# Strassen's seven block products for the feed-forward's gate and value, in a two-layer encoder kernel

## The reference

```python
h = layer_norm(DEEPNORM_ALPHA * h + m, ln_mix_g[layer], ln_mix_b[layer])   # m ends with "... @ w_out"
gate, up = jnp.split(h @ ffn_w_in[layer], 2, axis=-1)                      # w_in: 1024 x 5632
f = (jax.nn.silu(gate) * up) @ ffn_w_out[layer]                            # w_out: 2816 x 1024
h = layer_norm(DEEPNORM_ALPHA * h + f, ln_ffn_g[layer], ln_ffn_b[layer])
```

## Time and profile before

| | us |
|---|---|
| median of 3 runs | 2858.58 (2857.2 to 2860.23) |
| the profiled execution: its own time | 2860.23 |
| its span, first to last instruction | 2858.4 |
| PE busy (modelled) | 2659.3, 93% of the span |
| mean granted clock of PE | 0.963 of full speed |

### The profile page before, as it was taken

How to read it: one execution, slowest core, us unless ns; L and a number is a source line. 1 busy time by engine, 2 the same in 40 slices (tenths; PEclk the granted TensorE clock), 3 DMA queues, 4 the chain that set the end, 5 groups by cost and what they waited for, 6 DMA issues and landing times. The chain is left out here.

```text
span 2858.4 us, 34971 instructions
## 1 busy us (share of the span) xinstructions
PE 2659.3 (93%) x13476; PEld 2226.2 (78%) x13476; DVE 1420.3 (50%) x2523; ACT 556.6 (19%) x825; POOL 617.5 (22%) x448
## 2 busy tenths in 40 slices
PE   6787789999999999978999999995999999999996
PEld 5676678788888888767888888885878888888875
DVE  8699526532333322382667766666552333333227
ACT  3223232111111111112222222321211111111110
POOL 2968311111111121111111111110111111112210
PEclk9898899999999999989999999997999999999998
DMA  4333324112111111012010111101411121111101
GB/s 135 86 102 100 83 74 133 59 45 59 44 44 44 44 44 59 15 59 58 23 38 28 31 37 31 35 7 52 140 59 45 45 58 44 44 44 44 46 14 59
DMA packets 207701, 157.96 MB, mean 55 GB/s; under 512 B 15616, under 2 KB 189824, under 8 KB 206720
## 3 DMA queue, kind: packets, MB, share of 16 engines
q1 hardware_dynamic: 207616, 156.81, 18.0%
HBM read 139.02 MB, written 17.76 MB: 55 GB/s over the span
## 5 line engine op out<-in xcount | busy, mean ns | idle before, releaser
L588 DVE TENSOR_TENSOR h<-h,ps 128x512 f32<-128x512 f32 x320 | 219.5, 686 | 200.0 <-PE ps L365 199.6
L347 PE MATMUL ps<-aT_hi,w_hi 128*128 128x512 f32 x704 | 279.6, 397 | 3.0 <-DVE aT_lo L561 3.0
L347 PE MATMUL ps<-aT_hi,w_lo 128*128 128x512 f32 x704 | 277.5, 394 | 0.0
L347 PE MATMUL ps<-aT_lo,w_hi 128*128 128x512 f32 x704 | 275.1, 391 | 0.0
L1738 PE MATMUL ps<-aT_hi,w_hi 128*128 128x512 f32 x640 | 256.9, 401 | 1.7 <-PEq L241 1.7
L1738 PE MATMUL ps<-aT_hi,w_lo 128*128 128x512 f32 x640 | 251.5, 393 | 0.0
L1738 PE MATMUL ps<-aT_lo,w_hi 128*128 128x512 f32 x640 | 250.0, 391 | 0.0
L1710 POOL TENSOR_TENSOR w_lo<-w_raw,w_hi 128x1024 fp32r<-128x1024 f32 x38 | 91.7, 2419 | 555.7 <-ACT w_hi L62 555.7
L571 DVE TENSOR_TENSOR hgo_act_out<-hgo_act_out,ps 128x512 f32<-128x512 f32 x44 | 30.2, 687 | 352.5 <-ACT hgo_act_out L460 352.5
L571 DVE TENSOR_TENSOR s5o_act_out<-s5o_act_out,ps 128x512 f32<-128x512 f32 x44 | 30.2, 687 | 350.7 <-ACT s5o_act_out L460 350.7
L347 PEld LDWEIGHTS ps<-aT_hi,w_lo 128*128 128x128 f32 x704 | 133.2, 189 | 31.3
(11 more groups left out here) (324 smaller groups left out, 5919.4 us busy)
## 6 DMA issues: line engine op xcount, KB each, us to landing
w_raw<-in_ffn_w_in_dram SPq DMA_DIRECT2D x44, 512.0 KB, 5.0
w_raw<-in_hg_w_in_dram SPq DMA_DIRECT2D x40, 512.0 KB, 4.0
s5o_raw<-in_ffn_w_in_dram SPq DMA_DIRECT2D x22, 512.0 KB, 5.0
s5o_raw<-in_ffn_w_out_dram SPq DMA_DIRECT2D x11, 1024.0 KB, 5.2
hgo_raw<-in_ffn_w_in_dram SPq DMA_DIRECT2D x22, 512.0 KB, 5.0
hgo_raw<-in_ffn_w_out_dram SPq DMA_DIRECT2D x11, 1024.0 KB, 5.1
h<-in_x_dram SPq DMA_DIRECT2D x4, 1024.0 KB, 9.0
s_w_raw<-in_s_w_in_dram SPq DMA_DIRECT2D x8, 512.0 KB, 4.8
```

The lines of the kernel that those rows point to most:

```text
L347: ins = t.matmul(ps[:, 2 * b + a, :], w[q][:, a, kk, :], x[:, kk, rows], start=(kk == 0 and m == 0), stop=(kk == KT - 1 and m == 2))
L588: v.tensor_tensor(part, part, ps[:, 4 + m % 4, :], ALU.add).then_inc(S["out_acc"], 1)
```

## The change

Each hidden tile's gate and value is written as a 2x2 by 2x2 block product: weights by (gate or value, upper or lower four channel blocks), tokens by (channel half, token half). Seven block products of 12 matmuls replace the eight. `PRODUCTS` lists for each: first and second weight block with their operation, the token set, the PSUM bank (0 to 3).

- **Weights.** Each product has a set of its own: for the five sums, SP loads both blocks (256 KB each) into one of five slots (`SLOT_AT`), POOL adds or subtracts them, ACT makes the hi part, POOL the lo part; for the two plain ones ACT and DVE do it. Every load of a slot waits for the product that read it last. `w_out` comes as 512 KB for each tile, and DVE makes its lo part.
- **Tokens.** Five sums or differences of token blocks are made when a pair is turned (`keep_pair`): DVE forms them, ACT their hi parts, POOL their lo parts. Pairs are now token tiles (p, p + 4). The first product waits for all 20 lo parts.
- **Merging.** Ten DVE operations (`merge`) and three ACT copies (`keep`) a tile put the seven products together as banks come free; silu runs in place in SBUF. The hidden hi part moves from POOL to ACT.
- **Order.** A body of the loop is the products of tiles 2i+1 and 2i+2, then the outputs of group i. The last tile (21) stays at 96 matmuls, from six sets loaded during the last full outputs.
- **S5 stage.** On SP, `ungroup_y(n - 1)` comes behind `regroup_u(n + 1)`.

The core of the diff (of the three `body` functions the first is ACT's, the second DVE's, the third POOL's):

```diff
+    PRODUCTS = [((0, 0), (1, 1), ALU.add, "11+22", 0), ((1, 0), (1, 1), ALU.add, "11", 1),
+                ((0, 0), (0, 1), ALU.add, "22", 2), ((1, 1), None, None, "21-11", 3),
+                ((0, 0), None, None, "12-22", 0), ((0, 1), (1, 1), ALU.subtract, "21+22", 1),
+                ((1, 0), (0, 0), ALU.subtract, "11+12", 2)]
...
+    SLOT_AT = [0, 1, 2, 3, 4, 0, 1, 2, 3, 4, 0, 1, 2, 3]
...
+            def load_set(i, pos):
+                f, r = tile_at(i, pos)
+                if used_last(i, pos) is not None:
+                    s.wait_ge(S["product"], used_last(i, pos) + 1)
+                    carry(s, i)
+                fetch(plain_rows(pos), PRODUCTS[r][0], PRODUCTS[r][1], f, S[f"set_in{SLOT_AT[pos]}"])
...
+            turn_pair(PAIRS - 1)
+            t.wait_ge(S["x_set_lo"], 5 * PAIRS)
+            t.wait_ge(S["lo"], 2 * PAIRS)
+            unit(-1, 1)
...
+            def keep(f, n):
+                a.wait_ge(S["product"], f * NP + n + 1)
+                carry(a, f)
+                if n == 2:
+                    a.wait_ge(S["merged"], f * NMERGE + 4)
+                    carry(a, f)
+                elif not (isinstance(f, int) and f == 0):
+                    a.wait_ge(S["hid"], 2 * f)
+                    carry(a, f)
+                a.activation(act_out[0 if n == 0 else 1][:, :], ps[:, n, :], ACT.Copy).then_inc(S["kept"], 1)
...
+            def body(i):
+                hidden_hi(2 * i, 0, i)
+                w2_split(i, 0)
+                keep(2 * i + 1, 0)
+                keep(2 * i + 1, 1)
+                set_hi(i, 5)
+                keep(2 * i + 1, 2)
+                set_hi(i, 6)
+                w2_split(i, 1)
+                silu_late(2 * i + 1)
+                set_hi(i, 7)
+                silu_early(2 * i + 1)
+                set_hi(i, 8)
+                set_hi(i, 9)
+                hidden_hi(2 * i + 1, 1, i)
+                keep(2 * i + 2, 0)
+                keep(2 * i + 2, 1)
+                for pos in range(10, 13):
+                    set_hi(i, pos)
...
+            def body(i):
+                split_w2(i, 0)
+                merge_steps(2 * i + 1, range(1, 5))
+                split_w2(i, 1)
+                merge_steps(2 * i + 1, range(5, 11))
+                set_lo(i, 10)
+                merge(2 * i + 2, 1)
+                set_lo(i, 11)
+                merge_steps(2 * i + 2, range(2, 11))
+                accumulate(i, slice(0, 4))
...
+            def make_set(i, pos):
+                f, r = tile_at(i, pos)
+                g.wait_ge(S[f"set_in{SLOT_AT[pos]}"], 32 * uses(i, pos))
+                carry(g, i)
+                (hi, lo), (one, other) = set_rows(pos), plain_rows(pos)
+                g.tensor_tensor(other, one, other, PRODUCTS[r][2]).then_inc(S["set_sum"], 1)
+                g.wait_ge(S["set_hi"], index(i, pos) + 1)
+                carry(g, i)
+                g.tensor_tensor(lo, other, hi.bitcast(F32), ALU.subtract).then_inc(S["set_lo"], 1)
...
+            def body(i):
+                hidden_lo(2 * i, 0)
+                for pos in (5, 6, 7, 8, 9):
+                    make_set(i, pos)
+                hidden_lo(2 * i + 1, 1)
+                make_set(i, 12)
+                make_set(i, 13)
+                if not (isinstance(i, int) and i == LAST - 1):
+                    for pos in range(3):
+                        make_set(i + 1, pos)
...
                 if n == 0:
                     put_u(2)
-                else:
-                    ungroup_y(n - 1)
                 if 1 <= n < KT - 1:
                     regroup_u(n + 1)
+                if n >= 1:
+                    ungroup_y(n - 1)
```

More of the change, by code:

```diff
@@ L204, in project_and_feed @@
[L204 to L208, removed]
+    block_of = [k.first[:, :], k.hi0[:, :], k.lo0[:, :]] + [sb(f"x{n}", [P, PIECE], F32R)[:, :] for n in (3, 4, 5)]
+    plain_block = {n: k.plain[f"{tag}_x{n}"][:, :] for n in (3, 4, 5)}
@@ L498, in _ @@
-            if turns:
-                for tt in range(2, NT):
-                    keep_turned(NT + tt, tt)
+            for pos in range(NP, NP + 3):
+                set_hi(-1, pos)
+            for pair in range(PAIRS):
+                keep_pair(pair)
+            set_hi(-1, 10)
+            set_hi(-1, 11)
+            keep(0, 0)
+            keep(0, 1)
+            set_hi(-1, 12)
+            keep(0, 2)
+            set_hi(-1, 13)
+            silu_late(0)
+            set_hi(0, 0)
+            silu_early(0)
@@ new lines, in _ @@
+            body(0)
+            with a.Fori(1, LAST - 1) as i:
+                body(i)
+            body(LAST - 1)
+            for n, (_, second) in enumerate(LAST_SETS):
+                if second is not None:
+                    a.wait_ge(S["last_sum"], LAST_SUMS[n])
+                else:
+                    a.wait_ge(S[f"last_in{n}"], 32)
+                rows, raw_rows = last_set(n)
+                split_hi(a, rows[:, 0, :], raw_rows[:, 1, :]).then_inc(S["last_hi"], 1)
+            hidden_hi(2 * LAST, 0, LAST)
@@ L502, in _ @@
+            if turns:
+                for n in range(NT):
+                    keep_turned(n)
         @block.vector
@@ L620, in _, with body @@
-            group(0)
-            with v.Fori(1, NG - 2) as i:
-                group(i)
-            group(NG - 2)
-            product(LAST, 1)
+                    keep_pair(pair - 1)
+            keep_pair(PAIRS - 1)
+            set_lo(-1, 10)
+            set_lo(-1, 11)
+            merge_steps(0, range(1, 11))
+            set_lo(0, 3)
+            set_lo(0, 4)
+            def body(i):
+                split_w2(i, 0)
[7 more added lines that the diff above has]
+                accumulate(i, slice(0, 4))
+                if not (isinstance(i, int) and i == LAST - 1):
+                    set_lo(i + 1, 3)
+                    set_lo(i + 1, 4)
+                accumulate(i, slice(4, NT))
@@ L639, in _ @@
             if turns:
[L640 to L641 removed]
+                for n in range(4, NT):
+                    keep_turned(n)
         @block.gpsimd
@@ new lines, in _ @@
+            body(0)
+            with g.Fori(1, LAST - 1) as i:
+                body(i)
+            body(LAST - 1)
+            for n, (_, second) in enumerate(LAST_SETS):
+                (hi, lo), (one, other) = ([a[:, m, :] for m in range(2)] for a in last_set(n))
+                if second is not None:
+                    g.wait_ge(S[f"last_in{n}"], 32)
+                    g.tensor_tensor(other, one, other, ALU.add).then_inc(S["last_sum"], 1)
+                g.wait_ge(S["last_hi"], n + 1)
+                g.tensor_tensor(lo, other, hi.bitcast(F32), ALU.subtract).then_inc(S["last_lo"], 1)
```

628 lines of the change are left out of this document (371 added, 257 removed).

## The result

The changed kernel took 2912.01 us (median of 4 runs, 2908.02 to 2914.64) against 2857.89 for the kernel before (4 runs, 2854.99 to 2860.23): ratio 1.0189, 95% interval 1.0171 to 1.0206. It is 54 us slower; forecast were 2888 and "slower", with a range up to 2925. The profiled execution took 2908.02 us (span 2906.2), 47.8 more than the profiled one of before; all that follows accounts for these 47.8.

The account below looks back on a forecast made before the run. PE was taken to bound feed-forward groups, VectorE and PE both the middle norm. Layer 1 +14.5, layer 0 +17.0 and S5 -2.2 made +29.3 on the profiled 2860.2, giving a median of 2888 us; range 2843 to 2925.

Parts of the forecast that it names:

- turn of pair 0 to first product: Norm in the middle: first product waits for all token work and starts at 56.7 us, plus 1.4 for a slow turn.
- nine bodies: Feed-forward loop of each layer: nine periods of 64.3 us, against 65.8 before.
- last tile: End of outputs 9 to second outputs: shorter by 4.5 us in layer 0 and 7.0 in layer 1.
- The clock: Norm in the middle: longer PE idling slows a turn by 1.4 us and later products by about 2, +3.5 a layer.
- the walk: One loop body step by step: sets 7, 8, 9 each 0.6 us late, set 10 2.2 late; 60.3 becomes 64.3.
- The hand-overs: Between POOL and ACT in a summed set's round: about 0.08 us each, round 3.34; bounds 0.04 or 0.15.
- S5: S5 stage: regroup_u issued earlier shortens one PE wait, gaining 2.2 us once, bounds 0 and 3.
- The 9.4 us a layer for the exclusion: DVE operations with two SBUF inputs and POOL's sums block each other; without that each layer would be 9.4 us shorter.
- the short operations: Rival, faster: POOL's operations take 1.06 us, a body 62.6, total 2844; chance 0.13 together with all sets in time.
- the DMA rival: Rival, slower: loads of 512 KB a product set the pace, a body takes 68.6 us, total 2980; chance 0.06.
- the even case: Rival, about even: hand-overs and port waits at their low end, 14 us less a layer, total 2859; chance 0.12.
- All sets in time: Rival, faster: no product waits, 4.0 us more gained a body, some 2805; chance 0.13 together with the short operations.

Follow-up runs that it names:

- e3: Changed kernel with only POOL's order altered: in the body it sums the next set before making the rest of the current one; 2862.37 us.
- e4: Changed kernel with only ACT's order altered: roundings of plain sets 10 and 11 put ahead of the two keep copies; 2883.43 us.
- e8: Changed kernel without the five token sums, plain token blocks in their place (other values result); 2881.33 us.
- e6: As e5, with DVE's rest of w2 for the second tile moved behind merge 10; 2826.92 us, ratio to the kernel before 0.9886.
- e2: Changed kernel without POOL's weight sums in the loop's sets, all loads kept (other values result); 2832.24 us.
- e5: Changed kernel with the POOL order of e3, the ACT order of e4, and set 7's rounding ahead of a silu; 2823.31 us, ratio to before 0.988.
- e1: Changed kernel with the S5 stage's DMA order put back, ungroup_y ahead of regroup_u; 2916.08 us.
- e10: As e5, with the S5 stage's old DMA order put back; 2827.12 us, ratio to the kernel before 0.9888.
- e7: As e6, with DVE instead of POOL making two of the last pair's five token rests; 2818.58 us, ratio to the kernel before 0.9858.
- e9: As e5, with DVE instead of POOL making two of the last pair's five token rests; 2820.52 us, ratio to the kernel before 0.9866.

## Why the prediction was right, and by how much it was short

The direction was right, slower, and the time lies in the range; the size was short, +29.3 us against +47.8. By its steps, in the profiled execution:

| step | forecast | layer 0 | layer 1 |
|---|---|---|---|
| turn of pair 0 to first product, clock included | 58.1 | 57.3 | 57.4 |
| first product to first outputs, clock included | 69.0 | 70.5 | 67.6 |
| nine bodies | 578.7 | 586.5 | 586.5 |
| end of outputs 9 against before | +21.5 | +31.4 | +27.3 |
| last tile | -4.5 / -7.0 | -1.4 | -6.4 |

(The clock's 3.5 a layer is put in as 1.4 and 2.1.) 31.4 - 1.4 + 27.3 - 6.4 = 50.9, less 2.4 for an earlier begin of layer 0's feed-forward, leaves 48.5; measured were 47.8, so all else is 0.7 shorter. Forecast was 29.3. The prediction also took layer 1's 706.0 for both layers, where layer 0 had 704.6 before; that is 1.4 of the 18.5 missing.

**The step that was short is the body: 64.3 said, 65.1 measured.** Nine bodies in each layer make 15.6 us of the missing 18.5. The mechanism of the walk held, its sizes were short. A stall costs its shown idle time and 0.27, so in the body shown above set 7 cost 1.18, sets 8 and 9 0.73 and 0.70, and set 10 2.30, where the walk had 0.6, 0.6, 0.6 and 2.2.

*Set 7, the largest part.* The walk let DVE's rest of w2 end 16.4 us into the body and the set be ready at 19.8. The rest ended at 16.80 (2519.03) and the set was ready at 20.15 (2522.38), 3.35 later, as walked. PE began 0.13 behind that, a hand-over that the walk put at nothing. So the product started 1.06 late. The 0.4 lie in the steps in front of w2's rest: set 6 was ready at 15.7, not 15.2. The slower restart of PE, 0.11, is the rest of the 1.18, and of what set 10 cost over 2.2.

*The hand-overs.* 0.08 was estimated, 0.12 to ACT and 0.17 back were measured, so the round is 3.44 to 3.50, not 3.34; the upper bound of 0.15 was nearly it. Sets 8 and 9 cost the round less PE's 2.75, 0.7 each. Their restarts come not on top of that, since a later start of PE also makes it want the next set later.

*The clock.* The prediction charged it to the middle alone (turn 1.9 and first 48 matmuls 2.05 measured, 1.4 and 2 said). It also fell in one body a layer, 1.6 each, and within the first three tiles, for 10.2 us in layer 0 and 3.4 in layer 1; no step had either. That goes with the 2.9 us by which layer 0's first tiles took longer, of which 0.45 are longer waits; no run separates the two. Against that stands the ninth body, 63.95, in which the six last sets take the place of the next body's.

**Held by the traces:** POOL's operations at 1.27 to 1.32 for a set in the body, but for the sum that DVE held; the mechanism of both late places (e3 for the round, e4 for ACT's order, in part); the first product at 57.4, where 56.7 and 1.4 for the clock were said, of which e8 gives 14.8 to the token sums; outputs covered; the last tile in layer 1.

**The last tile in layer 0** gained 1.4 instead of 4.5. The second outputs were said to begin at 50.1 and began at 52.03 behind the end of outputs 9, and the kernel before began them at 53.4, not at the 54.6 that was worked back from an add. Most of the 1.9 is a slow turn again, in PE's timeline of the changed kernel:

```profile
1263.72 1.91 PE L416 MATMUL ps<-ident,h 128*128 128x128 f32 x16
...
1272.61 3.65 PE L416 MATMUL ps<-ident,h 128*128 128x128 f32 x16 [6.99 <-DVE aT_lo L772]
```

A turn behind 6.99 us of idle PE takes 3.65, where the one in front of it took 1.91. The prediction gave the slow turn to the middle alone. The clock was also at 0.50 for 3.4 us at the tile's begin, around a wait of 3.42 us. In e6 it wasn't, and with the same slow turn e6's second outputs began at 50.70, 1.3 sooner. So by estimate the clock took 3 us of this tile (1.7 and 1.3), and the rest of the walk was 1 too long: the two errors partly cancel.

**S5** was right at its place (1.9 to 2.3), and is not visible in the total.

**Two terms.** The load estimate of 3.8 us doesn't come out of its own figures: 5.0 less 512 KB at 290 GB/s is 3.2, and 3.3 is the median that the changed kernel's page gives. Nothing hangs on it, since set 5, the only one walked from its load, came in time. The 9.4 us a layer for the exclusion stands without its working, and no run here takes the exclusion away.

**Of the rivals**, the short operations fell with 1296 ns; the DMA rival fell with e2 and e5, where PE took the same loads with 121 GB/s, in e5 at its full pace; the even case wanted hand-overs at their low end. "All sets in time", put at some 2805 without an edit to bring it about, is what e5 does in the body: 60.45 against the ideal 60.3. The 2805 doesn't follow from the prediction's terms either: 18 bodies at 4.0 less are 72 us, so 2816, and with the first tiles at 57.7 instead of 66.9 2798. e5 took 2823. Its first tiles took 68.1 and 65.3, so not 57.7; its eighteen bodies sum to 4.0 more than 18 x 60.3, and layer 0's last tile gained 3.4 less than forecast.

**GpSimd against VectorE.** The Trainium skill (GPSIMD Engine Reference, section Engine selection) puts two-input elementwise work on VectorE, GpSimd being about twice as slow. The durations agree, 1296 ns against 686. But in e5 GpSimd makes all five sums of a tile with their rests and no product waits: 2 x 1.29 fit into 2.75. The measurement decides here, for the steady bodies; in the opening, where nothing covers it, two of five rests on DVE brought the first product forward by 2.24 us.

**Where the 115.4 us of removed matmuls went.** In e5 the nine bodies of layer 0 take 545.0 us and those of layer 1 544.4, 46.9 and 47.5 less than the 9 x 65.77 of before. Before, PE went from the turn of pair 0 to the first outputs in 90.9 and 92.3 us; e5 takes 125.5 and 122.7, 34.6 and 30.4 more, for the same outputs. So two thirds to three quarters of what the bodies save is paid before the first outputs, and the bodies of the change as it came saved only 9 x 65.77 - 586.5 = 5.4 us a layer.

## What to carry to other kernels

When an engine makes the operands of another in rounds that pass over a third engine, cost the round with its two hand-overs, and compare it with the consumer's period; if the engine's own operations fit into the period and the round doesn't, run it one item ahead. Fewer matmuls paid here only where they alone bounded the time: price what must be ready before the first one, once per layer, against what each repetition saves. In an in-order queue, look for copies that wait for a late producer and stand ahead of work that is ready; such reorderings add no work. Here they added up: 2.74 and 0.85 us a body alone, and 4.65 with a third.

## What the runs showed beyond what was expected

A stall of PE costs 0.27 us more than its idle time as shown: 48 matmuls took 11.26 behind one, 10.99 without. Of this 0.16 is the shown 0.39 of the matmul in front of it against the pace of 0.229, and 0.11 the slower restart.

Behind a stall of 1.9 to 2.03 us in an otherwise full stretch the granted clock fell to 1.2 GHz for some 3 us in a few of the bodies, costing 1.6, and not in the others with the same waits to 0.02 us. It was the second body of both layers in the changed kernel, the fourth in e8, the first, seventh or eighth, and last in e1; with 1.19 or less idle it was seen in none of e4's 18 bodies. What picks the body stays open.

In the opening the length of one wait differed between traces of the same feed-forward code: 3.37 us in e5 and 4.88 in e10. So a difference of 1 or 2 us there between two kernels that were profiled once each says little, and why e7 kept its 2.24 us and e9 didn't plainly do so stays open. Both waits have the same origin, SP's queue behind DVE's rest of w2.
